# Attention order, head sums in pairs and last rows by halves in a fused two-layer inference step

## The reference

```python
s = jnp.einsum('bqhd,bsd->bqhs', qi_b, keys_i)                     # 8 index heads
score = jnp.einsum('bqhs,bqh->bqs', jax.nn.relu(s), wi_b) * IDX_SCALE
top_s, top_i = lax.top_k(score, top)
...
bias = bias_tab[rel_bucket(top_i - pos_b[None, :, None])]
logits = jnp.einsum('bqgjd,bqkgd->bqgjk', q_b, k_sel) * ATTN_SCALE + jnp.moveaxis(bias, 2, -1)
probs = jax.nn.softmax(logits, axis=-1)
return jnp.einsum('bqgjk,bqkgd->bqgjd', probs, v_sel)
...
final, prev = lax.scan(step, init_state, ...)                      # SSM state of each stream
x = x + sqrelu_mlp(rmsnorm(x, norm_ffn[i]), mlp_w_up[i], mlp_w_down[i])
```

## Time and profile before

| | |
|---|---|
| median of three runs | 1895.78 us (1894.93 to 1898.64) |
| profiled execution | 1895.32 us, span 1893.4 us |
| mean granted clock of TensorE | 0.993 |
| PE busy | 1848.0 us, 98% |
| DVE busy | 1271.5 us, 67% |
| ACT busy | 801.7 us, 42% |
| POOL busy | 303.5 us, 16% |

### The profile page before, as it was taken

One profiled execution on the slowest core, in us unless ns is written; L12 is line 12 of the kernel. 1 busy time (PEld: TensorE's weight loads), 2 busy tenths in 40 slices (PEclk: granted clock), 3 DMA queues, 4 the chain that ended last, 5 costly groups with the idle time before them and its releaser, 6 DMA issues.

```text
span 1893.4 us, 35381 instructions
## 1 busy us (share of the span) xinstructions
PE 1848.0 (98%) x13223; PEld 1737.0 (92%) x13223; DVE 1271.5 (67%) x2357; ACT 801.7 (42%) x1435; POOL 303.5 (16%) x356
## 2 busy tenths in 40 slices
PE   8899899999999999999999999999999999999998
PEld 7777566899999999999999999999899999999998
DVE  4388875447758586447787888888554775858653
ACT  4232674334334343334465544656333434434332
POOL 0001651110000000022333343332112000000001
PEclk9999999999999999999999999999999999999999
DMA  6732203331322223322433444335423132222321
GB/s 154 128 74 53 64 24 125 77 95 57 112 62 73 84 78 94 97 55 82 129 101 123 130 133 133 102 122 164 148 67 110 51 112 62 83 75 87 92 68 56
DMA packets 311571, 176.88 MB, mean 93 GB/s; under 512 B 39888, under 2 KB 305040, under 8 KB 310416
## 3 DMA queue, kind: packets, MB, share of 16 engines
q1 hardware_dynamic: 308752, 172.49, 32.3%
q10 hardware_dynamic: 2688, 2.62, 0.5%
HBM read 155.18 MB, written 19.72 MB: 92 GB/s over the span
## 4 chain that ended last, share of the span: by engine, by line
PE 86%; DVE 4%; issue 4%; ACT 3%; DMA 1%; SPq 1%; DVEq 0%; POOL 0%; ACTq 0%
PE psum L206 29%; PE psum L1370 28%; PE psum L1398 14%; PE psum L589 1%; PE psum L2423 1%; PE psum L2436 1%; PE psum L2515 1%; PE psum L2450 1%; PE psum L565 1%; DMA W<-attn_w_in 1%; PE psum L593 1%; PE psum L554 1%; PE psum L542 1%; DVE conv_out L708 1%; PE psum L2354 1%
## 5 line engine op out<-in xcount | busy, mean ns | idle before, releaser
L206 PE MATMUL psum<-b2H,WH 128*128 128x320 f32 x912 | 218.2, 321 | 1.2 <-DVE xT L1616 0.9
L206 PE MATMUL psum<-b2H,WL 128*128 128x320 f32 x912 | 208.6, 310 | 0.0
L206 PE MATMUL psum<-b2L,WH 128*128 128x320 f32 x912 | 208.4, 310 | 0.0
L1370 PE MATMUL psum<-b2H,HT 128*128 128x320 f32 x816 | 186.2, 309 | 1.1 <-DVE xT L426 1.1
L1370 PE MATMUL psum<-b2L,HT 128*128 128x320 f32 x816 | 186.0, 309 | 0.0
L194 ACT ACTIVATE WH<-W 128x1024 fp32r<-128x1024 f32 x90 | 95.0, 1055 | 201.9 <-PE psum L206 161.5
L198 DVE TENSOR_TENSOR WL<-W,WH 128x1024 fp32r<-128x1024 f32 x90 | 139.7, 1552 | 55.8 <-ACT WH L194 54.9
L1398 PE MATMUL psum<-HH,HT 128*128 128x320 f32 x544 | 167.4, 308 | 1.5 <-DVE HL L1487 1.5
L1398 PE MATMUL psum<-HL,HT 128*128 128x320 f32 x544 | 167.8, 308 | 0.0
L206 PEld LDWEIGHTS psum<-b2H,WH 128*128 128x128 f32 x912 | 150.0, 190 | 16.0 <-issue 12.6
L206 PEld LDWEIGHTS psum<-b2L,WH 128*128 128x128 f32 x912 | 153.4, 189 | 0.0
(11 more groups left out here) (398 smaller groups left out, 4368.1 us busy)
## 6 DMA issues: line engine op xcount, KB each, us to landing
W<-ssm_w_in SPq DMA_DIRECT2D x98, 256.0 KB, 3.1
RW<-mlp_w_up SPq DMA_DIRECT2D x64, 256.0 KB, 3.0
RWx<-mlp_w_up SPq DMA_DIRECT2D x64, 256.0 KB, 3.0
RW<-mlp_w_down SPq DMA_DIRECT2D x64, 256.0 KB, 3.1
RWx<-mlp_w_down SPq DMA_DIRECT2D x64, 256.0 KB, 3.1
bc<-scratch_acs SPq DMA_DIRECT2D x8, 1280.0 KB, 7.5
W<-attn_w_in SPq DMA_DIRECT2D x32, 256.0 KB, 3.9
prev<-state_ssm SPq DMA_DIRECT2D x16, 512.0 KB, 5.3
```

What stands on the lines that cost most here:

```text
L206: last = pe.matmul(psum[0:m, 2 * b.slot + h, 0:TH], w[:, b.slot, k, 0:m], r[:, k, h * TH:(h + 1) * TH], start=(n == 0 and i == 0), stop=(n ...
L1370: last = pe.matmul(psum[:, i // 2 * 2 + h, 0:TH], w[:, k], x, start=(kx == 0 and c == 0), stop=(kx == 7 and c == 2))
```

## The change

It has seven parts, as the kernel runs.

1. **Start.** The 16 loads of the bias table leave the stretch between slabs 4 and 7 and stand in the loop over Q blocks (2, 2, 3, 3, 3 and 3 of them, with 0 to 5). The constants `rep` and `cfar` are gone; the far bias is taken off the table instead (`onehot[half - 1] -= 1.0`).
2. **Q blocks.** The index products of two samples stand side by side in `Rs`, and one `sum_heads` sums both, in two 32-column tiles; one copy and two stores follow, in every second block.
3. **Prompt attention.** `spread_sums` moves ahead of the logits and alternates between the two 64-column tiles; `copy_spread` and `scale_heads` come one unit later; the copies of turned probabilities go in pairs where a tile has one or two key blocks; heads are kept in float32 (`hF`), and `heads_hi` and `heads_lo` leave the loop.
4. **Sample attention.** The mask goes by DRAM to `MS`, POOL adds it to the bias (`BMs`), and the mask's matmuls on PE are gone. `heads_hi(b)` and `heads_lo(b)` of tile b stand in step b.
5. **Output projection to MLP 0.** The last output block has PSUM banks 6 and 7, and the last row of MLP 0 bank 4 and 5, instead of banks still to be emptied.
6. **SSM.** `pe_sample_states` works on four groups of 32 rows (256 columns each, banks 4 to 7), and waits for `copy_prev(u,p)`; ACT's second SiLU comes after the first `copy_prev`; DVE's first `sample_states` comes earlier.
7. **End.** The last row of MLP 1 is computed in halves of 320 tokens (`last_row_pe`), each added and squared for itself; the samples' output is scaled by ACT and DVE half each, and stored from ACT.

```diff
-            load_slab(sp, Block(4), slab_g1(4))
-            sp.wait_ge(tb_out, 16)
...
-            for p0 in range(0, 64, DS):
-                load_bias_p(p0)
-            load_slab(sp, Block(5), slab_g1(5))
...
+            for b in range(5, 8):
+                load_slab(sp, Block(b), slab_g1(b))
...
+                if b < 6:
+                    for n in range((0, 2, 4, 7, 10, 13)[b], (2, 4, 7, 10, 13, 16)[b]):
+                        load_bias_p(DS * n) if n < 8 else load_bias_s(n - 8)
```

```diff
+            def sum_heads(i, bank_=7):
+                pe.wait_ge(iR, 2 * i + 3)
+                for s in range(2):
+                    pe.matmul(psum[32 * s:32 * s + 32, bank_, 0:512], sel[:], Rs[:, s, 0:512], start=True, stop=True)
...
                 turn(u + 1)
+                if u % 8 == 0 and u:
+                    spread_sums(u // 8 - 1)
                 if u + 4 < NU:
                     logits(u + 4)
                     logits(u + 5)
-                if u % 8 == 0 and u:
-                    spread_sums(u // 8 - 1)
```

```diff
                     out = psum[:, 2 * a + lo // 512, 0:n]
-                    pe.matmul(out, repst[:], maskS[:, lo:lo + n], start=True, stop=False)
-                    last = pe.matmul(out, qst[:, a], kpT[:, a, lo:lo + n], start=False, stop=True)
+                    last = pe.matmul(out, qst[:, a], kpT[:, a, lo:lo + n], start=True, stop=True)
...
+            def load_mask(b):
+                sp.wait_ge(bm, NU + max(2 * b - 2, 0))
+                sp.dma_start(MS[:, b % 2],
+                             skew(S["scores"], DS * b * KEYS_S, [[0, 8], [KEYS_S, DS], [1, KEYS_S]])
+                             ).then_inc((ss_in, bias_in)[b % 2], 16)
...
+                    pool.tensor_tensor(BMs[:, a], MS[:, b % 2], biasS[:, a], ALU.add).then_inc(bm, 1)
```

```diff
-        for k in range(2):
-            r = slice(64 * k, 64 * k + 64)
-            last = pe.matmul(bank(4 + k), xddt[r, p, SEQ:T], Bx[r, 4 * k:4 * k + 4].rearrange("p b n -> p (b n)"),
+        for i in range(4):
+            r = slice(32 * i, 32 * i + 32)
+            last = pe.matmul(psum[:, 4 + i, 0:256], xddt[r, p, SEQ:T], Bx[r, 2 * i:2 * i + 2].rearrange("p b n -> p (b n)"),
                              start=True, stop=True)
...
+        for h in range(2):
+            for i in (2, 3):
+                n, b = n0 + i, ((0, 3), (4, 5))[i % 2][h]
...
+            last.then_inc(sw_mm, 1)
+            if h == 0:
+                final_sums(pe)
```

More of the change, by code:

```diff
@@ L72, in shape_constants @@
     c[:, 640:648] = i[:, None] // DS == np.arange(DB)[None, :]
[L73 to L77, removed]
+    sel = np.zeros((P, 32), np.float32)
     sel[i, i % DS] = 1.0
@@ L205, in chunk_products @@
             for h in range(2):
-                last = pe.matmul(psum[0:m, 2 * b.slot + h, 0:TH], w[:, b.slot, k, 0:m],
+                last = pe.matmul(psum[0:m, b.out + h, 0:TH], w[:, b.slot, k, 0:m],
                                  r[:, k, h * TH:(h + 1) * TH],
@@ L417, in build, with in_pair, turned_bank, turned_free @@
     NPV = NU // 2
+    def in_pair(u):
+        return UNITS[u][1] <= 1
+    def turned_bank(u):
+        return 4 + (u // 2 % 2 if in_pair(u) else u % 2)
+    def turned_free(u):
+        last = max(p for p in range(u // 2 * 2) if turned_bank(p) == turned_bank(u))
+        return last // 2 * 2 + 2 if in_pair(last) else last + 1
     LAST_PAIR = 3
@@ L1378, in rows_pe, with last_row_pe @@
                 final_turn_early(pe)
+                last_row_pe(pe)
+                return
+    def last_row_pe(pe):
+        n0 = op0(63)
+        pe.wait_ge(sw_rx, 14)
+        for i in (2, 3):
+            pe.wait_ge(sw_lo, n0 + i + 1)
+        for h in range(2):
+            for i in (2, 3):
+                n, b = n0 + i, ((0, 3), (4, 5))[i % 2][h]
+                for k in range(4):
+                    for c, (w, x) in enumerate(((HT[h_tile(n)], HH), (HT[h_tile(n)], HL), (LT[l_tile(n)], HH))):
+                        last = pe.matmul(psum[:, 2 + h, 0:TH], w[:, k], x[:, b, k],
+                                         start=(i == 2 and k == 0 and c == 0), stop=(i == 3 and k == 3 and c == 2))
+            last.then_inc(sw_mm, 1)
+            if h == 0:
+                final_sums(pe)
     def down_bank(g, i):
@@ L1764, in mlp_act @@
                 down_act(act, g, end)
-        next_act(act, layer, 7)
+        if layer:
+            act.wait_ge(acc_done, 38)
+            for h in range(2):
+                act.wait_ge(sw_rx, 16 + h)
+                act.activation(SQ[:, 1, h * TH:(h + 1) * TH], x_half(7, h), ACT.Square).then_inc(sq_ready, 1)
+        else:
+            next_act(act, layer, 7)
         if layer == 0:
@@ L1811, in final_pe, with final_squares @@
             pe.matmul(psum[:, 0, t:t + 1], ACC[:, t * P:(t + 1) * P], ones[:], start=(t == 0), stop=False)
+    def final_squares(pe, half):
+        pe.wait_ge(sq_ready, 40 + half)
+        for t in ((0, 1), (2, 3, 4))[half]:
+            last = pe.matmul(psum[:, 0, t:t + 1], SQ[:, 1, t * P:(t + 1) * P], ones[:], start=False, stop=(t == NT - 1))
+        return last
+    def final_pe(pe):
+        final_squares(pe, 0)
         pe.wait_ge(newton, 16 + 7)
@@ L1814, in final_pe @@
             y_turn(pe, t, ORD[6])
-        pe.wait_ge(sw_rx, 16)
-        for i in range(4):
+        pe.wait_ge(sw_rx, 17)
+        final_squares(pe, 1).then_inc(x_turn, 1)
+        for i in range(KC - 1):
             y_turn(pe, 2, ORD[i])
[L1818 to L1821, removed]
         for i in range(4, KC - 1):
@@ L3077, in _ @@
             dve.wait_ge(qz, 4)
-            sample_step(0)
-            with dve.Fori(1, DB - 1) as b:
+            for b in range(DB):
                 sample_step(b)
-            sample_step(DB - 1)
             sample_heads_lo(DB - 1)
```

392 lines of the change are left out of this document (209 added, 183 removed).

## The result

The changed kernel takes 1912.42 us (median of 5 runs, 1908.37 to 1914.51) against 1895.34 us of the kernel before (5 runs); the ratio is 1.0085 with an interval of 1.0068 to 1.0102. It is 17 us slower, outside the predicted range (1883 to 1907). Its profiled execution has a span of 1910.8 us, 17.4 more than before.

The account below looks back on a forecast made before the run. PE's own list was taken to bound the kernel (busy 98%). Savings at six places against +14.8 and +10 us in the sample attention summed to +1.8 us on the profiled 1895.3: 1897 us, range 1883 to 1907.

Parts of the forecast that it names:

- Start, -7.5: Start: PE's waits for slabs and the low clock behind them go once bias loads move; 7.5 us saved (6.5 to 8).
- Q blocks, -5.1: Q blocks: eight sums become four of 1.05 us and a 1.32 us wait goes; 5.1 us saved.
- Prompt attention, -1.3: Prompt attention: filled exponent waits against new stops at seven seams; 1.3 us saved, ends at -4 and +3.
- I take these as nearly level: Prompt attention: filled exponent waits about cancel new stops of up to 2 us at seven seams; net -1.3 us.
- The rival with seven stops and falls of the clock: Prompt attention seams: seven 2 us stops, +3 in place of -1.3, three clock falls at 2.5; 1909 us; chance 0.1.
- Sample attention, +14.8 and +10: Sample attention: steps lengthen from 7.03 to 9.4 us, +14.8 us; clock falls behind the stops add +10 (4 to 15).
- the chain: Sample attention: keys' copy, heads_hi, heads_lo, normalization, second maximum in sequence; PE stops 2.9 us per full step.
- four falls at 2.5 us: Sample attention: the clock falls in four of six long steps, up to 2.5 us each; +10 us.
- Output projection and MLP 0, -2.0: Output projection to MLP 0: two waits for xT (1.1 and 0.9 us) go by using other banks; 2.0 us saved.
- SSM, -4.9: SSM: four 32-row groups run together save 6.1 us, less 1.2 for a last-group wait; -4.9 (-6 to +12).
- the new wait of the last group: SSM, last group: a matmul waits for copy_prev and comes 2.2 us later, against 1.0 saved; +1.2 us.
- End, -2.2: End: last row's addition, square and column sums and the samples' output scaling in halves; 2.2 us saved.

Follow-up runs that it names:

- the seventh experiment: Changed kernel with both head splits early, scale_heads one unit earlier, SSM's small loads in MLP 0, two start products and last copy_prev earlier: 1857.87 us.
- The fourth experiment: Changed kernel with copy_spread and scale_heads one unit earlier in the prompt attention, sample attention as it was: 1896.50 us.
- the first experiment: Changed kernel with heads_hi moved right behind sample_turned on ACT and heads_lo ahead of the first sample_max on DVE: 1883.19 us.
- the third experiment: Changed kernel with only ACT's heads_hi moved, to right behind sample_turned; DVE's heads_lo stays ahead of the normalization: 1884.28 us.
- the second: Changed kernel with three needless matmuls on PE ahead of each turn_sample_heads but the last: 1901.71 us.
- the ninth experiment: Kernel of the seventh experiment with the SSM's state products back on two groups of 64 rows, 512 columns each: 1865.06 us.

## Why the prediction was wrong

**Start, -7.5: mis-sized, -4.75.** The wait for the slab went, with its low clock. I had priced the moved bias-table matmuls at 0.3. The step that failed is the new order of the first products, which the list of the change leaves out and to which the sum gave no price: `first_products(0, 7)` now stands ahead of the norm's spread, so PE gets to it earlier than its low part, which stands behind DVE's steps for the norm, and stops for 1.81 us, with low clock behind it. With that stop repaired (the seventh experiment) the start ends 9.0 us earlier than before, so the gains themselves were larger than 7.5.

**Q blocks, -5.1: right,** -6.0. A sum of two samples takes 1.03 us (176.73 to 177.76), with 1.05 reckoned.

**Prompt attention, -1.3: the step that failed first.** "I take these as nearly level" set gains against stops of up to 2 us at seven seams. No row stood behind that number, and it was a guess. The stops came as described, 13.2 us in all, and the low clock behind six of them. The rival with seven stops and falls of the clock, with a chance of 0.1, had the mechanism; it put the stage at +3 and 7.5 of clock, and +4.7 was measured. The fourth experiment shows the size of what I had called level: 15.9 us. The gain of the rest, which filled the exponents' waits, was larger than I thought as well: without the shift by one unit the stage is 11.1 us shorter than before (86.1 in place of 97.2). So the term was wrong on both sides, and its net error of 6.0 is the smaller for it.

**Sample attention, +14.8 and +10: right in mechanism,** 27.9 measured. The stop was 3.24 us against 2.9 (DVE's low part took 1.20 us, not 0.78). The first and the third experiment show the chain, the second splits the sum: 15.7 us came with the chain against 14.8, and 12.3 with the clock against 10. I took four falls at 2.5 us; there were seven, at about 1.8 us in a full step. That the product came near is partly luck: the count was too small and the price too high.

**Output projection and MLP 0, -2.0: +1.1.** The waits for `xT` went. What I left out is that the projection can start at the lower clock: its first block has rows of 0.73 us until 374.7, one every 0.53 us in place of 0.29, which costs some 2.5 us of the 5.5. The four blocks up to the matmuls on `conv_in` take 30.8 us in place of 28.3. The clock had been at 0.50 since 365, behind the stop of 1.74 us. It is not shown that all of this belongs to the long stops: in the first experiment, which has none of them, the block starts at 0.50 too, for 3 us, behind two waits of 1.07 and 0.99 us, while behind the same two waits it starts at the upper level in the seventh. The other 0.6 us of the error have no cause shown.

**SSM, -4.9: right,** -5.4, and the new wait of the last group came as reckoned (2.56 us against 2.2). The Trainium skill (TensorEngine Tiling (Array Packing), Key Properties) says that different tiles can run their weight loads and matmuls in parallel; the ninth experiment agrees, at 7.2 us.

**End, -2.2: -0.1.** The halves of the last row have PE take the sums of squares between them (1893.15 to 1894.18), where it had done them while DVE added. The steps behind the row became shorter by 1.0 us, from 4.48 (1879.49 to 1883.97) to 3.50 (1897.75 to 1901.25), and that is what the sums cost (1.03 us).

The sum of the errors is 15.6 us: 6.0 in the prompt attention, 3.1 each in the sample attention and in the projection, 2.75 at the start, 2.1 at the end, less 1.4 in the Q blocks and the SSM. Four of the five that went against the forecast hold low clock: in the sample attention I had priced it a little low, in the other three at nothing.

## What to carry to other kernels

An instruction that waits for nothing is not free: put it where its engine idles, and not behind an instruction that waits for the last thing in a step. One copy of 0.6 us on ACT, standing behind the copy of the next keys, cost 28 us over eight steps. When new stops of PE are expected, add to their length what the low clock may take from the dense work behind them: here stops of 1.7 to 3.2 us brought it down in nearly every place. Filling a stop with needless matmuls can pay where the stop itself can't be taken away.

## What the runs showed of the hardware

- A stop of 1.81 us was enough to bring the granted clock to 0.50 for about 7 us of fully busy PE (at 30 us), and so was a stop of 2.15 us at 238 us, while the clock stayed at 1.00 behind another of 2.15 us at 222. Two waits of 1.07 and 0.99 us close together were followed by 0.50 in one kernel (first experiment, 338 us) and by the upper level in another (seventh). Which stops do it was not settled.
- A step with three needless matmuls is 1.8 us shorter than without: 9.64 against 11.45.
- Four 32-row groups of float32 matmuls of 256 columns take 0.65 us together, and two 64-row groups of 512 columns 1.06.
- Small loads of 16 KB or less, still being issued when the output projection began, went with stops of PE of 4.6 to 5.9 us in three kernels, and cost 9.3 us in the clearest case; with the same loads issued 7 to 9 us ahead of it, in three others, the profile has no such stop.
